# Weight blocks in six half places instead of three whole ones, in a one-core hybrid decoder layer

## The reference

```python
h = rmsnorm(x, g_mix)
proj = h @ w_in                      # 1024 -> 3*512 qkv | 512 z | 16 | 2*512 glu
q, k, v = silu(short_conv(qkv)); o = gated_delta_rule(q, k, v, g, beta, s0)   # chunked, inverse of I + L
cv = silu(group_norm(depthwise_conv31(glu)))
x = x + concat(o, cv) @ w_out
x = x + square(relu(rmsnorm(x, g_mlp) @ w_up)) @ w_down      # 1024 -> 4096 -> 1024
x = x + (p_emb @ w_ple) * sigmoid(rmsnorm(x, g_ple) @ w_ple_gate)
y = rmsnorm(x, g_final)
```

## Time and profile before

| | |
|---|---|
| median of 3 runs | 1814.85 us (1811.62 to 1817.52) |
| profiled execution: its time, its span | 1815.31 us, 1813.5 us |
| mean granted TensorE clock | 0.951 |
| TensorE matmul busy | 1619.3 us, 89% |
| VectorE busy | 1042.2 us, 57% |
| ScalarE busy | 749.3 us, 41% |
| HBM traffic over the span | 84 GB/s |

### The profile page before, as it was taken

The page is one execution under the profiler, slowest core; times in us unless marked ns, Lnnn a source line. Parts: engine busy times, 40 slices in busy tenths (PEclk is TensorE's granted clock), DMA queues, the critical chain, the costliest instruction groups (busy, mean ns, idle before and its releaser), DMA issues.

```text
span 1813.5 us, 27026 instructions
## 1 busy us (share of the span) xinstructions
PE 1619.3 (89%) x11162; PEld 1405.8 (78%) x11162; DVE 1042.2 (57%) x1707; ACT 749.3 (41%) x1192; POOL 65.6 (4%) x68
## 2 busy tenths in 40 slices
PE   4998866899989997877899999987999999999987
PEld 2786656888978775654677777766989999999987
DVE  3755699678763665779655554455334343434543
ACT  5556523344355424532224243354543242414454
POOL 0000000000000040000000000000000000000000
PEclk9999897899999989888899999999999999999999
DMA  6353222322233332312221213323323333233322
GB/s 181 87 146 102 66 79 65 84 81 77 65 104 82 78 87 68 90 47 64 59 68 45 65 52 91 98 83 117 101 83 93 88 88 94 82 94 87 92 70 82
DMA packets 281023, 153.33 MB, mean 85 GB/s; under 512 B 36996, under 2 KB 272636, under 8 KB 280893
## 3 DMA queue, kind: packets, MB, share of 16 engines
q1 hardware_dynamic: 279879, 150.32, 29.3%
q10 hardware_dynamic: 1022, 1.28, 0.3%
HBM read 135.03 MB, written 16.97 MB: 84 GB/s over the span
## 4 chain that ended last, share of the span: by engine, by line
PE 68%; DVE 16%; ACT 8%; issue 4%; DMA 3%; ACTq 0%; SPq 0%; POOL 0%; DVEq 0%; POOLq 0%
PE ps L1299 55%; DVE of L1964 3%; DVE prod L1883 3%; PE ps L1435 2%; DVE Xp L1884 2%; DVE w_lo L1634 2%; PE ps L1464 2%; PE ps L1458 1%; PE ps L1413 1%; DVE tk L1856 1%; ACT L919 1%; DMA w_raw<-in_w_up 1%; PE ps L1282 1%; PE ps L1425 1%; ACT w_hi L915 1%
## 5 line engine op out<-in xcount | busy, mean ns | idle before, releaser
L915 ACT ACTIVATE w_hi<-w_raw 128x1024 fp32r<-128x1024 f32 (+3 forms) x258 | 232.6, 902 | 320.1 <-DMA w_raw<-in_w_down 175.8
L1299 PE MATMUL ps<-hh_hi,w_hi 128*128 128x256 f32 (+1 forms) x960 | 322.4, 336 | 29.0 <-DVE w_lo L1634 23.2
L1299 PE MATMUL ps<-hh_lo,w_hi 128*128 128x256 f32 (+1 forms) x960 | 314.9, 328 | 0.0
L1299 PE MATMUL ps<-hh_hi,w_lo 128*128 128x256 f32 (+1 forms) x960 | 314.3, 327 | 0.0
L1634 DVE TENSOR_TENSOR w_lo<-w_raw,w_hi 128x1024 fp32r<-128x1024 f32 (+3 forms) x258 | 266.7, 1034 | 55.1 <-ACT w_hi L915 54.3
L1299 PE MATMUL ps<-u_hi,w_hi 128*128 128x512 f32 (+2 forms) x768 | 260.3, 339 | 28.6 <-DVE w_lo L1634 14.2
L1299 PE MATMUL ps<-u_lo,w_hi 128*128 128x512 f32 (+2 forms) x768 | 252.7, 329 | 0.0
L1299 PE MATMUL ps<-u_hi,w_lo 128*128 128x512 f32 (+2 forms) x768 | 252.2, 328 | 0.0
L1299 PE MATMUL ps<-hm_hi,w_hi 128*128 128x512 f32 (+5 forms) x600 | 211.1, 352 | 27.2 <-ACT yb L961 9.8
L1299 PEld LDWEIGHTS ps<-hh_hi,w_hi 128*128 128x128 f32 x960 | 184.8, 193 | 52.9 <-DVE w_lo L1634 34.1
L1299 PE MATMUL ps<-hm_lo,w_hi 128*128 128x512 f32 (+5 forms) x600 | 201.1, 335 | 0.0
(11 more groups left out here) (274 smaller groups left out, 2254.1 us busy)
## 6 DMA issues: line engine op xcount, KB each, us to landing
w_raw<-in_w_up SPq DMA_DIRECT2D x64, 512.0 KB, 4.0
w_raw<-in_w_in SPq DMA_DIRECT2D x48, 512.0 KB, 4.2
w_raw<-in_w_down SPq DMA_DIRECT2D x64, 256.0 KB, 2.7
w_raw<-in_w_down SPq DMA_DIRECT2D x32, 512.0 KB, 4.0
w_raw<-in_w_out SPq DMA_DIRECT2D x16, 512.0 KB, 4.0
w_raw<-in_w_ple_gate SPq DMA_DIRECT2D x16, 512.0 KB, 4.1
qt<-qkv_dram SPq DMA_DIRECT2D x8, 768.0 KB, 5.2
xin<-in_x_prompt SPq DMA_DIRECT2D x8, 512.0 KB, 6.3
```

The source lines that it names most:

```text
L915: nc.scalar.activation(w_hi[job.slot][:, 0:job.kts, 0:job.m], w_raw[job.slot][:, 0:job.kts, 0:job.m], ACT.Copy).then_inc(w_hid, 1)
L1299: last = nc.tensor.matmul(dst, wt[job.slot][:, k, 0:m], x[:, k, lo:hi], start=(i == 0 and n == 0), stop=(end and n == 2), skip_group_check ...
```

## The change

The region of the three whole places is divided into six half places of 2 KB per partition each for the raw (later lo) and the hi part. A job takes `ceil(kts/4)` neighbouring places, so a whole block takes two and the down blocks of half 0 and the ple blocks take one. `lay_out` gives each job its place and the last earlier holder of it (`after`), and `weight_plan` puts its load in slot 2*after+1 and both its splits in one slot, chosen from estimated times between 3.0 and 1.9 half jobs before the job begins. Where a run of whole blocks follows one of whole blocks, load and ScalarE's split keep their slot; 100 of the 258 loads stand in an earlier slot than before, none in a later one. VectorE's split now stands behind the side stages of its slot instead of ahead of them. (The first two jobs stay as they were.)

```diff
+RING = 6
+def lay_out(jobs):
+    place, holder, loads = 0, [None] * RING, [0] * RING
+    for job in jobs:
+        need = -(-job.kts // 4)
+        if place + need > RING:
+            place = 0
+        job.place, job.after = place, None
+        for n in range(place, place + need):
+            if holder[n] is not None and (job.after is None or holder[n].j > job.after.j):
+                job.after = holder[n]
+            holder[n] = job
+        loads[place] += 1
+        job.load = loads[place]
+        place = (place + need) % RING
+def weight_plan():
+    for job in JOBS:
+        begins = TIMES[2 * job.j - 1] if job.j else 0.0
+        issue = -3.0
+        if job.after is not None:
+            loads[2 * job.after.j + 1].append(job)
+            issue = TIMES[2 * job.after.j + 1]
+        at = min(max(issue + 1.5, begins - 3.0), begins - 1.9)
+        h = 0
+        while h < SLOTS and TIMES[h] <= at:
+            h += 1
+        job.early = job.j < 2
+        if not job.early:
+            splits[h].append(job)
...
-                if h % 2 and h // 2 + 3 < len(JOBS):
-                    load_w(JOBS[h // 2 + 3])
+                for job in LOADS[h]:
+                    load_w(job)
...
-                if h % 2 and h // 2 + 2 < len(JOBS):
-                    split_hi(JOBS[h // 2 + 2])
+                for job in SPLITS[h]:
+                    split_hi(job)
                 for stage in SIDE[h]:
...
-                if h % 2 == 0 and h // 2 + 1 < len(JOBS):
-                    split_lo(JOBS[h // 2 + 1])
+                if h == 0:
+                    split_lo(JOBS[1])
                 for stage in SIDE[h]:
                     if stage[0] in stages:
                         stages[stage[0]](*stage[1:])
+                for job in SPLITS[h]:
+                    split_lo(job)
```

More of the change, by code:

```diff
@@ L108, in plan @@
     for j, job in enumerate(jobs):
-        job.j, job.u, job.slot = j, u, j % 3
+        job.j, job.u = j, u
         u += job.n
+    lay_out(jobs)
     return jobs
+RING = 6
[13 more added lines that the diff above has]
+        place = (place + need) % RING
 JOBS = plan()
@@ L134 @@
 TIMES = slot_times()
+def weight_plan():
+    loads, splits = [[] for _ in range(SLOTS)], [[] for _ in range(SLOTS)]
+    for job in JOBS:
[11 more added lines that the diff above has]
+            splits[h].append(job)
+    return loads, splits
+LOADS, SPLITS = weight_plan()
 def evictions():
@@ L469, in build @@
         gls = at(CR, "gls", [P, CT, DB, HIST + DS])
-        w_raw = [at(WR, f"w_raw{s}", [P, KT, P], off=8192 * s) for s in range(3)]
-        w_lo = [at(WR, f"w_lo{s}", [P, KT, P], F32R, off=8192 * s) for s in range(3)]
-        w_hi = [at(WR, f"w_hi{s}", [P, KT, P], F32R, off=8192 * s + 4096) for s in range(3)]
+        held = lambda n: [P, min(KT, 4 * (RING - n)), P]
+        w_raw = [at(WR, f"w_raw{n}", held(n), off=2048 * n) for n in range(RING)]
+        w_lo = [at(WR, f"w_lo{n}", held(n), F32R, off=2048 * n) for n in range(RING)]
+        w_hi = [at(WR, f"w_hi{n}", held(n), F32R, off=2048 * (RING + n)) for n in range(RING)]
         raw = [at(TR, f"raw{n}", [P, QH + TS[1]]) for n in range(2)]
@@ L564, in build @@
         ld_i, ld_c, ld_g, ld_h, ld_d = (sem(n) for n in ("ld_ident", "ld_consts", "ld_gain", "ld_vectors", "ld_heads"))
-        ld_w = [sem(f"ld_w{n}") for n in range(3)]
+        ld_w = [sem(f"ld_w{n}") for n in range(RING)]
         st_yb = [sem(f"st_yb{n}") for n in range(3)]
@@ L682, in load_w @@
             def load_w(job):
-                dst = w_raw[job.slot][:, 0:job.kts, 0:job.m]
+                dst = w_raw[job.place][:, 0:job.kts, 0:job.m]
                 i = job.i
@@ L690, in load_w @@
                        "gate": lambda: w_gate[:, i * P:(i + 1) * P], "ple": lambda: w_ple[:, i * P:(i + 1) * P]}[job.kind]()
[L691 to L694, removed]
+                if job.after is not None:
+                    sp.wait_ge(mm, job.after.u + job.after.n)
+                sp.dma_start(dst, src.rearrange("(k p) c -> p k c", p=P)).then_inc(ld_w[job.place], 16)
             def spill(dram, kind, s, j):
@@ L913, in split_hi @@
             def split_hi(job):
-                act.wait_ge(ld_w[job.slot], 16 * (job.j // 3 + 1))
-                nc.scalar.activation(w_hi[job.slot][:, 0:job.kts, 0:job.m], w_raw[job.slot][:, 0:job.kts, 0:job.m],
+                act.wait_ge(ld_w[job.place], 16 * job.load)
+                nc.scalar.activation(w_hi[job.place][:, 0:job.kts, 0:job.m], w_raw[job.place][:, 0:job.kts, 0:job.m],
                                      ACT.Copy).then_inc(w_hid, 1)
@@ L1298, in multiply @@
                     for n, (wt, x) in enumerate(((w_hi, rhs[0]), (w_hi, rhs[1]), (w_lo, rhs[0]))):
-                        last = nc.tensor.matmul(dst, wt[job.slot][:, k, 0:m], x[:, k, lo:hi], start=(i == 0 and n == 0),
+                        last = nc.tensor.matmul(dst, wt[job.place][:, k, 0:m], x[:, k, lo:hi], start=(i == 0 and n == 0),
                                                 stop=(end and n == 2), skip_group_check=job.kind == "out")
@@ L1633, in split_lo @@
                 dve.wait_ge(w_hid, job.j + 1)
-                nc.vector.tensor_tensor(w_lo[job.slot][:, 0:job.kts, 0:job.m], w_raw[job.slot][:, 0:job.kts, 0:job.m],
-                                        w_hi[job.slot][:, 0:job.kts, 0:job.m].bitcast(F32), ALU.subtract).then_inc(w_lod, 1)
+                nc.vector.tensor_tensor(w_lo[job.place][:, 0:job.kts, 0:job.m], w_raw[job.place][:, 0:job.kts, 0:job.m],
+                                        w_hi[job.place][:, 0:job.kts, 0:job.m].bitcast(F32), ALU.subtract).then_inc(w_lod, 1)
             def heads(t):
```

## The result

The changed kernel takes 1847.88 us (median of 4, 1844.47 to 1850.33), the kernel before 1814.19 in the same comparison: 1.0183 of its time, interval 1.016 to 1.0207. That is 33 us slower, where 14.7 us faster was forecast and 1812 was the end of the range. The profiled execution has a span of 1848.5 us, 35.0 more than before.

A forecast was written before the change was run, and what follows sets the result against it. TensorE was taken as the bound, so only its idle time and slow-clock matmuls counted. Gains of 25.9 us less losses of 11.2 gave −14.7 on 1815.3, so 1800.5 us; range 1788 to 1812.

The forecast's parts named there:

- (j): First down block of each group: another job's split stands ahead of `u_lo`, TensorE waits longer; 9.4 us lost.
- third rival: The clock drops behind the waits at the group starts: 12 us more, about 1812; chance 0.13.
- (c): Second gate of half 0: its 3.19 us wait shrinks only by its own split; 1.2 us gained.
- (d): Last two down blocks and first gate of half 0: splits made a slot earlier, ahead of row sums; 2.3 us gained.
- (k): Second gate block of half 1: `w_lo` stands ahead of `hh_lo` and `acc`; with half 0's like place, 1.8 us lost.
- (f): Gates of half 1: the 0.44 us waits after six ple evictions go; 2.6 us gained.
- (b): Last gate block of half 0: loaded ahead of x rows, ending the 7.04 us wait and slow clock; 9.1 us gained.
- (h): Nine `w_lo` waits, 605 to 1090 us: three outside the inverses give 2.6 us, six among the inverses nothing.
- (e): Up blocks following eight down blocks: half places come free sooner, two waits of 0.9 go; 1.9 us gained.
- (g): `onr` waits at 936 and 1033 us: an up block's earlier load shortens ScalarE's delay; 2.9 us gained.
- (a): Five gates of half 0 and half 1's first out block: `w_lo` made a slot earlier; 3.3 us gained.
- slower side: Group starts: `w_hi` also waits for its load, and the clock drops; 28 us more, about 1828; chance 0.07.

The follow-up runs named there:

- starts_only: loads_only with only the second to fourth down blocks' splits of each half 0 group (24 jobs) as in the changed kernel: 1833.04 us, 1.0084 of the kernel before.
- loads_only: The changed kernel's half places and early loads, with both weight splits where the kernel before had them: 1808.05 us, 0.9955 of the kernel before.
- runs 6 to 8: loads_only with splits of jobs 0 to 57, 58 to 145, or 146 on as in the changed kernel: 1809.18, 1831.76 and 1821.25 us.
- first_gate_moved: loads_only with the splits of jobs 146 to 157 alone as in the changed kernel: 1817.2 us, 1.0 of the kernel before.
- second_gates_moved: loads_only with the splits from job 170 on (all of half 1) as in the changed kernel: 1811.51 us, 0.9983 of the kernel before.
- rows_later: loads_only with the x and sample row loads four slots later, behind the first out block's load of half 1: 1808.41 us, 0.9949 of the kernel before.
- gates_moved: loads_only with the splits of jobs 158 to 167 (gates and ple of half 0) as in the changed kernel: 1807.34 us, 0.9948 of the kernel before.
- filled: The changed kernel with eight added 512-column matmuls at each of eight group starts, into the next unit's PSUM bank: 1832.7 us, 1.0082 of the kernel before.

## Why the prediction was wrong

**The step that failed is (j)**, the group starts: "+1.25 in six groups", "1.9" at 708, nothing at 816, together 9.4 us. The mechanism was right in its place and its engines: the fourth down block's split, its ScalarE part behind `u_hi`, VectorE standing at it with `u_lo` behind. It was sized wrongly twice.

First the waits. Those for `u_lo` grew by 14.1 us, since the eighth start was not free (9.67 instead of 7.85) and those at 626, 899 and 992 grew by 2.2, 1.7 and 2.8. (j) counted one split at these three; the changed kernel has a second one there, 0.60 us ahead of the last up block's `yb`. At 1077, 1123 and 1170, where the 1.25 was worked out, they grew by 1.38, 1.12 and 1.13.

Second, the clock fell behind them. starts_only prices the whole at 23 us over loads_only; its `u_lo` waits are 11.8 us longer, so some 11 us are matmuls at the low clock (the estimate from the granted clock is 14 for this pair of traces, 11 to 17 over all). I had written that term down as 0 to 14 and then set it off against the `onr` waits, at nothing. The price of one drop, "2.0 at most", was too low too: at 708 the clock is 0.50 over the whole 12 us behind the wait. The kernel before showed such a drop already: at a group start, behind a wait of 1.36 us, 12 matmuls take 4.52 us, and the text did not use that row. The third rival ("the clock drops behind the waits at the group starts", 12 us) came true, but it was only a part.

What lies between the forecast of -14.7 and the measured +33 us, by the runs: (j) 23 for 9.4, 14 us; (c) and (d) together +7 for -3.5, 10; (k) and (f) together +5 for -0.8, 6; (b) 0.7 for 9.1, 8 by the trace; (h) 1. That is 39 of 48. The rest is as large as what the parts of runs 6 to 8 leave open, and stays open with it.

**(d) and (k), the ends of the halves, had the wrong sign or size.** (d) counted 2.3 gained, (k) 1.8 lost. first_gate_moved costs 8 us (1.1 of it the last group's start), second_gates_moved 5. I looked at which split was late, not at what the split newly stands ahead of: in the last down blocks the `xT` eviction, and `hh_lo`, on which the gate's product depends directly, k by k. (k) named `hh_lo` but traced it only to `rs`: it foretold 4.5 us for the wait behind the first ple block of half 1, which stayed at 3.07 (3.06 before), while TensorE stood 1.51 us for `hh_lo` in the first gate.

**(b) moved its wait.** Load order and landing came as predicted; the next load in the queue, the ple block's, took the x rows' delay, and in the changed kernel its split held a gate's eviction: 0.7 of 9.1 us gained (by the trace; no run moves the splits of jobs 168 and 169 alone). With the old splits the same load order gains 5.9 at the gate and gives 2.75 back at the out block, of which rows_later returns 1.6. The prediction said "nobody waits for them", of the x rows, and did not ask who is queued behind them. The Trainium skill (DMA: Bandwidth & Descriptors, Queues, rings and completion order) says that a queue has one ring on each DMA engine, and that an engine takes a ring's descriptors in order. The trace agrees with the order, in both directions: the gate's load ahead of the rows lands in 4.3 us (8.8 before), the ple block's behind them in 9.1.

**(c), (e), (g) were right, and (a) for its five gates.** In the changed kernel the waits of 0.54 at the gates of half 0 are gone (at the first out block, which (a) counted too, TensorE stands 1.40 us instead of 0.54), the second gate's is 2.12 instead of 3.19, the two of 0.9 at up blocks are gone, `onr` waits are 1.73 and 1.72 instead of 3.30. loads_only keeps (e) and (g), gates_moved (a) besides; neither has (c), whose wait is 3.19 and 3.21 there.

**(f) was wrong for the most part:** of the six waits of 0.44, 2.6 us, five came back one block on, at the ple block, with 1.8 us.

**(h) was near in size, not in kind.** No gain in the inverses was right; the three waits outside, 6.9 us, became waits of 5.2 us for the eviction on the same queue, which the prediction named as one of two things that would make it wrong; the other, half-clock stretches behind (j), came too. Waits of TensorE from 620 to 1115 us in the changed kernel:

```profile
PE ps L1342 <- DVE u_lo L1791: 24.2, 7, 9.7
...
PE ps L1342 <- DVE xT L1713: 14.8, 8, 3.5
```

The earlier trace rows has 20.4 us for `w_lo` there; 14.8 for `xT` stand in their place.

**The slower side** was given 0.07, as one mechanism with a price of 28 us. It was to come from late loads at the group starts; it came from the clock there, from the ends of the halves and from the late gate, none of them enough alone. The measured 1848 lies above every rival, 20 us above the slowest. The Trainium skill (TensorE: Matmul & The Clock Gate, Part 1: The HAM clock gate) says that activity is what lifts the clock. filled agrees: keeping TensorE at work through the wait took about 16 us off the other matmuls.

## What to carry to other kernels

An in-order engine's early work is not free: before a step is moved ahead on its queue, list what is queued behind it at its new place and ask whether it can itself stand waiting there; a step that isn't needed for three half jobs belongs behind the one that TensorE needs next. Price a wait of TensorE in the main product with its length plus the matmuls at a lower clock that can follow it (here behind six of eight waits), and where a wait can't be avoided, matmuls into a free bank can keep the clock. When two things change together, run each alone first: here one half gained 8 us and the other lost 41.

## What was not expected of the hardware

Added work made the kernel faster: 64 matmuls of 512 columns, 15.8 us of them, took 15 to 18 us off the changed kernel, which with them is still 15 us slower than the kernel before. The 2.52 us wait in starts_only was followed by 12 matmuls in 5.42 us, though three matmuls and small products of the delta rule lay between. And the clock differs between executions where the waits are the same: the traces of gates_moved and rows_later have the same kernel as loads_only up to 1150 us and the same idle time of TensorE up to there within 1.1 us, and are 8 and 11 us later there, so a difference of pace of that size between two single traces proves nothing, while most waits at the same place agree to 0.1 or 0.2 us (not all: the one for `u_lo` at 708 is 0.22 to 1.92 us in these three).
